# A decoder layer's expert gates: a table in HBM filled by indirect DMAs, in place of one-hot products

## The reference

```python
q = (xc @ wq).reshape(tc, H, 2, PEER_HALF)             # 8 heads, two halves of a key
s = einsum('thpd,hpnd->thpn', q, subkeys)               # 2 x 128 scores for a head and token
sv, si = top_k(s, K)                                    # 16 best of each half
cand = sv[:, :, 0, :, None] + sv[:, :, 1, None, :]      # 16 x 16 sums
cidx = si[:, :, 0, :, None] * NK + si[:, :, 1, None, :]
best, pos = top_k(cand, K)                              # 16 best pairs (i, j)
eidx = take_along_axis(cidx, pos, axis=-1)
gates = softmax(best)
act = gelu(einsum('td,thkd->thk', xc, u_tab[eidx]))
y = einsum('thk,thkd->td', gates * act, v_tab[eidx])
```

## Time and profile before

| | us |
|---|---|
| median of 3 runs | 1065.33 (1064.71 to 1065.81) |
| the profiled execution, its own time | 1063.1 |
| its span, first to last instruction | 1061.4 |
| PE busy | 1039.0 (98%) |
| DVE, ACT, POOL busy | 718.4, 520.2, 326.6 |
| HBM read, written | 202.15 MB, 2.10 MB |
| mean granted TensorE clock | 0.99 of full |

### The profile page before, as it was taken

The page is one execution under the profiler, slowest core; times in us unless marked ns, Lnnn a source line. Parts: engine busy times, 40 slices in busy tenths (PEclk is TensorE's granted clock), DMA queues, the critical chain, the costliest instruction groups (busy, mean ns, idle before and its releaser), DMA issues.

```text
span 1061.4 us, 18274 instructions
## 1 busy us (share of the span) xinstructions
PE 1039.0 (98%) x7154; PEld 963.8 (91%) x7154; DVE 718.4 (68%) x1601; ACT 520.2 (49%) x797; POOL 326.6 (31%) x161
## 2 busy tenths in 40 slices
PE   8999999889999999999999999999999999999996
PEld 8999889889999999999999999988888888888875
DVE  7778887964897069556666767765555756666556
ACT  5686657335444454544434343355544555455542
POOL 1000000001888788866666666600001000000002
PEclk9999999988999999999999999999999999999999
DMA  9878748544555555544444444456669567776651
GB/s 360 325 242 307 246 139 314 165 137 160 179 176 180 177 175 182 187 158 137 143 140 140 139 140 140 140 177 193 193 192 334 180 205 250 235 240 205 195 174 42
DMA packets 57413, 205.43 MB, mean 194 GB/s; under 512 B 6768, under 2 KB 8816, under 8 KB 56560
## 3 DMA queue, kind: packets, MB, share of 16 engines
q1 hardware_dynamic: 55616, 199.01, 57.0%
q0 software_dynamic: 1424, 5.24, 1.3%
q10 hardware_dynamic: 288, 0.01, 0.0%
HBM read 202.15 MB, written 2.10 MB: 192 GB/s over the span
## 4 chain that ended last, share of the span: by engine, by line
PE 91%; DVE 4%; ACT 1%; issue 1%; DMA 1%; SPq 0%; ACTq 0%; DVEq 0%
PE px L1079 33%; PE pw L786 16%; PE pw L787 16%; PE pw L788 15%; PE px L1051 5%; DMA ada<-in_ada 1%; DVE w_lo L1130 1%; PE px L1017 1%; PE px L786 1%; PE px L787 0%; PE px L788 0%; PE px L850 0%; ACT w_hi L487 0%; PE px L947 0%; PE pw L1099 0%
## 5 line engine op out<-in xcount | busy, mean ns | idle before, releaser
L487 ACT ACTIVATE w_hi<-raw 128x1024 fp32r<-128x1024 f32 x312 | 328.5, 1056 | 334.0 <-PE px L1079 168.8
L786 PE MATMUL pw<-a_hi,w_hi 128*128 128x256 f32 x1280 | 370.0, 289 | 2.1 <-DVE a_lo L1391 2.1
L787 PE MATMUL pw<-a_lo,w_hi 128*128 128x256 f32 x1280 | 362.6, 283 | 0.0
L788 PE MATMUL pw<-a_hi,w_lo 128*128 128x256 f32 x1280 | 362.5, 283 | 0.0
L420 POOL TENSOR_TENSOR w_lo<-raw,w_hi 128x1024 fp32r<-128x1024 f32 x128 | 307.5, 2403 | 142.2 <-ACT w_hi L487 140.9
L1130 DVE TENSOR_TENSOR w_lo<-raw,w_hi 128x1024 fp32r<-128x1024 f32 x184 | 224.5, 1229 | 156.0 <-ACT w_hi L487 155.3
L786 PEld LDWEIGHTS pw<-a_hi,w_hi 128*128 128x128 f32 x1280 | 245.8, 192 | 3.8 <-DVE a_lo L1391 2.5
L787 PEld LDWEIGHTS pw<-a_lo,w_hi 128*128 128x128 f32 x1280 | 246.1, 192 | 0.1
L788 PEld LDWEIGHTS pw<-a_hi,w_lo 128*128 128x128 f32 x1280 | 245.8, 192 | 0.0
L1079 PE MATMUL px<-w_hi,ws_hi 128*128 128x512 f32 x512 | 159.3, 390 | 0.9 <-DVE ws_lo L1543 0.9
L1079 PE MATMUL px<-w_lo,ws_hi 128*128 128x512 f32 x512 | 159.0, 389 | 0.0
(11 more groups left out here) (328 smaller groups left out, 1118.0 us busy)
## 6 DMA issues: line engine op xcount, KB each, us to landing
raw<-in_u SPq DMA_DIRECT2D x128, 512.0 KB, 3.7
raw<-in_v SPq DMA_DIRECT2D x128, 512.0 KB, 4.6
raw<-in_ws SPq DMA_DIRECT2D x56, 512.0 KB, 4.9
ada<-in_w_ada SPq DMA_DIRECT2D x32, 512.0 KB, 7.1
ada<-in_ada SPq DMA_DIRECT2D x6, 1024.0 KB, 11.1
raw<-in_w SPq DMA_DIRECT2D x7, 768.0 KB, 11.2
ada<-in_ada SPq DMA_DIRECT2D x4, 512.0 KB, 7.0
xT<-in_xT SPq DMA_DIRECT2D x8, 128.0 KB, 10.4
```

The costliest lines, as they stand in the source:

```text
L487: return nc.scalar.activation(out, in_, ACT.Copy, **kw)
L786: nc.tensor.matmul(out, lh, rh, start=start and x == 0, stop=False)
L787: nc.tensor.matmul(out, lh, rl, start=False, stop=False)
L788: last = nc.tensor.matmul(out, ll, rh, start=False, stop=stop and x == len(pairs) - 1)
```

## The change

The gates no longer pass through one-hot products. A table of 128 x 128 x 256 floats (16.8 MB) is kept in HBM, ordered j, i, token. POOL clears it in 32 DMAs of 512 KB from a zero tile of 256 floats a partition, each tied to a count of low parts made in the blocks. The place of a choice in the table is (j x 128 + i) x 256 + token; DVE works it out for each unit. The units go in another order (two heads of tile 0, then the same heads of tile 1), in groups of four, each with its exp. When the gates of a group are ready, POOL issues 64 indirect DMAs, one for each unit and each of the 16 choices: each adds 128 floats (one for a token) to their 128 places in the table, and a unit waits until the additions of the unit before of the same tile have landed. SP waits for all additions before it loads the first row of the table and the first piece of V; then each row of V brings a table row of 128 KB (128 runs of 1 KB) with it, in a ring of four. DVE multiplies it into the row of W (`gate_w`) ahead of the split.

POOL keeps the low parts of U's pieces 0 to 15. DVE makes those of 16 to 127; its unit is cut into six steps, and one low part goes ahead of each. ACT only runs gelus in U, with four exps, after groups 6, 20, 32 and 44. PE's one-hots and transposes are gone.

```diff
-GA_U = 31
-OH = T // 4
-SCORES_AFTER = (4, 8, 11, 15)
-ENDS_AFTER = (18, GA_U - 2)
+UNITS = TT * PH
+SCORES_AFTER = (7, 12, 17, 22)
+POOL_PIECES = 16
+PER_UNIT = 6
+EXP_AFTER = (6, 20, 32, 44)
+ZERO = 256
+ZERO_DMAS = 32
...
 
+            def load_gates(r):
+
+                if r >= RING:
+                    sp.wait_ge(w_gated, r - RING + 1)
+                sp.dma_start(g_row[:, r % RING], gates_d[r * P * T:(r + 1) * P * T].rearrange("(i t) o -> i (t o)", i=P)) \
+                    .then_inc(g_landed[r % RING], 16)
+
             for m in range(UP, VP + NK):
+                if m == VP:
+                    for t in range(TT):
+                        sp.wait_ge(scattered[t], 16 * PH * TOPK)
+                    for r in range(RING):
+                        load_gates(r)
                 load_piece(m)
                 r = m - VP
+                if r >= RING:
...
 
+            table = gates_d.rearrange("(n i f) o -> n i (f o)", i=P, n=ZERO_DMAS)
+
+            def clear(first, last):
+
+                for n in range(first, last):
+                    pool.wait_ge(lo_ready, 4 + 46 * n // ZERO_DMAS)
+                    pool.dma_start(table[n].rearrange("i (a f) -> i a f", f=ZERO),
+                                   zero[:, :].unsqueeze(1).broadcast_to([P, NK * T // ZERO // ZERO_DMAS, ZERO])) \
+                        .then_inc(zero_landed, 16)
+
+            pool.wait_ge(zero_ready, 1)
+            clear(0, 9)
             pool.wait_ge(aT_copied, TT)
             nc.gpsimd.affine_select(out=aT[:, :, :, :].rearrange("p a h t -> p (a h) t"),
                                     in_=aT[:, :, :, :].rearrange("p a h t -> p (a h) t"),
                                     compare_op=ALU.is_ge, fill=0.0, base=0,
                                     pattern=[[0, TT * HG], [1, P]], channel_multiplier=-1).then_inc(aT_ready, 1)
+            clear(9, 25)
 
             pool.wait_ge(mod2_done, 1)
             pool.wait_ge(gt1_done, 1)
             nc.gpsimd.memset(keys[:, :, :], 0.0).then_inc(keys_cleared, 1)
+            clear(25, 28)
 
             for t in range(TT):
                 pool.wait_ge(xn_ready[t], 2)
             pool.dma_start(x1_d.rearrange("(a p) n -> p a n", p=P), x1[:, :, :]).then_inc(x1_spilled, 16)
+            clear(28, ZERO_DMAS)
 
             pool.wait_ge(lo_ready, UP)
-            for m in range(UP, VP):
+            for m in range(UP, UP + POOL_PIECES):
                 split_lo(m)
 
+            pool.wait_ge(zero_landed, 16 * ZERO_DMAS)
+            for c in range(PH // 2):
+                pool.wait_ge(gate_ready, c + 1)
+                for h in range(2):
+                    for t in range(TT):
+                        if 2 * c + h:
+                            pool.wait_ge(scattered[t], 16 * TOPK * (2 * c + h))
+                        i = 4 * c + 2 * t + h
+                        for k in range(TOPK):
+                            nc.gpsimd.indirect_dma_start(gates_d, bass.IndirectOffsetOnAxis(ap=place[:, i, k:k + 1], axis=0),
+                                                         gate[:, i, k:k + 1], None, compute_op=ALU.add) \
+                                .then_inc(scattered[t], 16)
 
             pool.wait_ge(piece_used, VP + E_ROWS)
             pool.wait_ge(x1_spilled, 16)
...
 
 
-            for g in range(GA_U):
+            def split_w(v):
+
+                act.wait_ge(w_gated, v + 1)
+                if v >= RING:
+                    act.wait_ge(piece_used, VP + v - RING + 1)
+                copy(ws_hi[:, v % RING], W[:, v]).then_inc(wsplit_hi, 1)
+
+            for g in range(NG):
                 if g == 8:
                     act.wait_ge(x1_spilled, 16)
+                if g == NG - 1:
+                    for r in range(RING):
+                        split_w(r)
                 split_hi(UP + 2 * g + 4)
                 act.wait_ge(piece_used, UP + 2 * g + 2)
                 nc.scalar.activation(W[:, 2 * g:2 * g + 2], pw[g % 2][:, :].rearrange("p (j t) -> p j t", j=2), ACT.Gelu) \
                     .then_inc(u_out, 1)
                 split_hi(UP + 2 * g + 5)
-                for t in range(TT):
-                    if g == ENDS_AFTER[t] - 1:
-                        q = slice(t * PH, (t + 1) * PH)
-                        act.wait_ge(best_ready, t + 1)
+                for c in range(PH // 2):
+                    if g == EXP_AFTER[c]:
+                        q = slice(4 * c, 4 * c + 4)
+                        act.wait_ge(best_ready, c + 1)
                         nc.scalar.activation(gate[:, q], gate[:, q], ACT.Exp).then_inc(gate_exp, 1)
-                    if g == ENDS_AFTER[t]:
-                        act.wait_ge(idxT_done, t + 1)
...
@@ -1007,14 +1027,15 @@
                 after(b)
 
 
-            def scores(t, c):
-
-                if t == 0:
+            def scores(n):
+
+                c, t = divmod(n, TT)
+                if n < 4:
                     pe.wait_ge(act_took, evac_count(WQ + c))
                 else:
-                    pe.wait_ge(score_used, 2 * c + 2)
+                    pe.wait_ge(score_used, 2 * (n - 4) + 2)
                 for h in range(2):
-                    last = nc.tensor.matmul(px[c][:, h * T:(h + 1) * T], qpT[:, 2 * c + h, t * P:(t + 1) * P],
+                    last = nc.tensor.matmul(px[n % 4][:, h * T:(h + 1) * T], qpT[:, 2 * c + h, t * P:(t + 1) * P],
                                             keys[:, 2 * c + h], start=True, stop=True)
                 last.then_inc(score_done, 1)
 
...
-                    elif g - 2 < GA_U:
+                    else:
                         pe.wait_ge(u_out, g - 1)
-                    else:
-                        pe.wait_ge(u_gated, g - 1 - GA_U)
                 columns_piece(m, pw[g % 2][:, e * T:(e + 1) * T])
 
...
-            def one_hots(n):
-
-                pe.wait_ge(oh_ready, n + 1)
-                if n >= 4:
-                    pe.wait_ge(g_lower_taken, n - 3)
-                    pe.wait_ge(g_upper_taken, n - 3)
-                for y in range(4):
-                    last = nc.tensor.matmul(px[n % 4][:, y * P:(y + 1) * P], oh_i[n % 2][:, y], oh_j[n % 2][:, y],
-                                            start=True, stop=True)
-                last.then_inc(oh_used, 1)
...
-                scores(0, c)
-            for g in range(GA_U):
+            for n in range(4):
+                scores(n)
+            for g in range(NG):
                 for e in range(2):
                     u_piece(g, e)
                 if g in SCORES_AFTER:
-                    scores(1, SCORES_AFTER.index(g))
-                if g in ENDS_AFTER:
-                    transposed(ENDS_AFTER.index(g))
-            for g in range(GA_U, NG):
-                for e in range(2):
-                    u_piece(g, e)
-                    n = 2 * (g - GA_U) + e
-                    if n < OH:
-                        one_hots(n)
+                    scores(4 + SCORES_AFTER.index(g))
 
             def v_part(v, t, halves=(0, 1)):
 
...
+            def gates(c):
+
+                q = slice(4 * c, 4 * c + 4)
+                need(at["last"])
+                v.tensor_tensor(gate[:, q], best[:, q], best[:, q, 0:1].broadcast_to([P, 4, TOPK]), ALU.subtract) \
                     .then_inc(best_ready, 1)
+                for t in range(TT):
+                    ins = v.tensor_scalar(place_f[:, 2 * t:2 * t + 2], ij[:, 0, 4 * c + 2 * t:4 * c + 2 * t + 2], float(T),
+                                          token[:, t:t + 1], ALU.mult, ALU.add)
+                need(go(ins))
+                v.scalar_tensor_tensor(place[:, q], ij[:, 1, q], float(P * T), place_f[:, :, :], ALU.mult, ALU.add)
+
+            def normal(c):
+
+                q = slice(4 * c, 4 * c + 4)
+                dve.wait_ge(gate_exp, c + 1)
+                need(go(v.tensor_reduce(gsum[:, q], gate[:, q], AX, ALU.add)))
+                need(go(v.reciprocal(ginv[:, q], gsum[:, q])))
+                v.tensor_tensor(gate[:, q], gate[:, q], ginv[:, q].unsqueeze(2).broadcast_to([P, 4, TOPK]),
                                 ALU.mult).then_inc(gate_ready, 1)
 
+            dve.wait_ge(zero_landed, 16 * ZERO_DMAS)
+            for i in range(4):
+                for step in steps:
+                    step(i)
+            gates(0)
+            upper_half(4)
+            lower_half(4)
+            normal(0)
+            dve.wait_ge(lo_ready, UP + POOL_PIECES)
+            m = UP + POOL_PIECES
+            for i in range(4, UNITS):
+                for n, step in enumerate(steps):
+                    split_lo(m)
+                    m += 1
+                    if i > 4 or n > 1:
+                        step(i)
+                    if i > 4 and i % 4 == 0 and n == 4:
+                        normal(i // 4 - 1)
+                if i % 4 == 3:
+                    gates(i // 4)
+            while m < VP:
+                split_lo(m)
+                m += 1
+                if m == UP + POOL_PIECES + PER_UNIT * (UNITS - 4) + 5:
```

(64 more changed lines are left out.)

157 lines of the change are left out of this document (34 added, 123 removed).

## The result

The changed kernel takes **1206.37 us** (median of 4 runs, 1201.99 to 1208.31), against 1065.05 for the kernel before (4 runs, 1064.71 to 1065.81): a ratio of 1.132, 95% interval 1.1289 to 1.1352. The forecast of 1014 (1004 to 1024) was wrong, and so was its sign. It is rival 2, further out than I had priced it. The profiled execution took 1206.38 with a span of 1204.6.

A forecast was written before the change was run, and what follows sets the result against it. PE was taken as the bound, busy 98% of the span with 91% of the chain. 1063.1 - 57.4 (one-hots, transposes) + 3 (clears) + 3 (V) = 1011.7; the runs' median lies 2.2 higher: forecast 1014, range 1004 to 1024.

The forecast's parts named there:

- rival 2: SP's wait before V: scatter late, p over 1.43, V starting at 314.6 + 256 p + 12.5; 1108 to 1152; chance 0.28.
- The chain of work: In U, one-hots add plainly to PE's path; removing them and the transposes saves 57.4 us, and DVE's low parts fit.
- p: Time per indirect DMA that POOL issues for the scatter, 256 in all: taken as 1.0 us.
- My upper bound: Upper p for POOL's indirect DMAs: 0.88 for a plain DMA plus 0.89 of blocking by DVE, 1.77 us.
- The threshold: Before V: last issue over by 629.9, 12.5 us ahead of V's first matmul, allowing p up to 1.21 us.
- The clears: In the blocks before U, 32 DMAs of 512 KB clearing the table: cost taken as 3 us, between 0 and 11.
- V: In V, DVE's gate products and the table rows: cost taken as 3 us, between 0 and 15.
- The rule on the shared port: DVE and GpSimd share an SBUF port pair by exclusive lock, so each indirect DMA could wait out a low part.
- Rival 1: Before V: scatter late but still faster, p between 1.21 and 1.43; 1031 at p 1.3; chance 0.16.
- Rival 3: DVE in U or table rows in V set the cadence: 11 and 29 us, together 1024 to 1051; chance 0.07.
- Rival 4: On PE: the change brings nothing, its time being filled otherwise; within 0.2%, chance 0.03.

The follow-up runs named there:

- kernel 1: The changed kernel with every second of the 16 choices left out, so 128 indirect DMAs in place of 256: 1010.47 us.
- the second table: kernel 1 with a second table of the same size added, cleared beside the first and read by nobody: 1028.84 us.
- experiment 6: The changed kernel with VectorE's low parts for U's pieces 16 to 127 cut to 64 of 1024 columns: 1177.76 us.

## Why the prediction was wrong, point by point

**The chain of work was right.** One-hots were an addition to PE's stream: U fell from 429.2 to 372.0 us, against 429.2 less the forecast 57.4 = 371.8. PE waits for no low part in U, so VectorE carries 112 of them beside top-k, as worked out.

**The step that failed is p**, the price of an indirect DMA, taken as 1.0 and bounded at 1.77, with 1.21 as the most that the forecast could bear. It measured 1.965, and V's first matmul came at 835.25 instead of near 645. In parts, from the experiments: 0.97 for the DMA with 128 places and a plain write; 0.59 for the addition; 0.30 between two DMAs; and 0.10 for VectorE's low parts beside it (1.965 - 1.86). The plain DMAs of the earlier trace rows were the wrong neighbours in three ways. They gave 0.88, near the 0.97, but by size, and size is not what is paid. The addition was mentioned and not priced by itself. And the gap of 0.30 appears in no row of a lone DMA, so a string of them was priced without it. My upper bound put the blocking of the earlier trace rows on every DMA, which turned out nine times too much, and still fell short, since it had neither the addition nor the gap.

**The threshold was right.** The prediction asked for the last issue over by 629.9, thus started by some 628; the runs put the knee at a last start of 626.5 to 628. The 12.5 us from there to V's first matmul measured 13.0. With the measured price, rival 2's own formula gives V's start as 314.6 + 256 x 1.965 + 12.5 = 830.1, against 835.25 on the chip; 5 of that 5.15 are the first gates, ready at 319.7 in this execution, and 315.1 in kernel 1. The time by it would be 1063.1 + (830.1 - 699.8) + 6 + 2.2 = 1201.6, against 1206.37. So the rival was right in place and mechanism, and its formula gives the size once p is known; but it had a chance of 0.28, and its highest p of 1.77 gives only 1152.

The first 4 us, by which the first score is late (271.0 against 266.7), fit TensorE's clock. Between 10 and 20 us the granted clock was 0.57 here and 0.83 in the kernel before, with the same work (here, then before):

```profile
10.00:20.00 10.00, 7.73 (x39) 0.57 1.01 416
```

```profile
10.00:20.00 10.00, 7.55 (x50) 0.83 1.02 417
```

The kernel with ten choices had 0.58 there and kernel 1 had 0.83, with the same code up to that point, so it goes by the execution and not by the change. By 213 us that is 2.8 us (213.34 against 210.59 for the same matmuls, of L992 here and of L972 before). The other 1.6 arise between 210 and 250 us, where the clock was low again (0.51 from 240 to 250, where before had 0.73).

**The clears**, taken as 3 (0 to 11), cost nothing that shows (266.5 against 266.7). The count of idle DMA time was too strict, as if no ring of pieces absorbed anything, but it had the two places where the second table breaks through.

**V**, taken as 3 (0 to 15), cost 1.2 in kernel 1. In the changed kernel V's matmuls span 1193.1 - 835.2 = 357.9, 5.8 over before's 352.1. Two waits of PE are 2.5 of it. One, of 0.73 us at 955.83, ends a wait for a table row issued at 941.59, just behind the loads of the end's constants, as the prediction had feared. The other, of 1.72 at 985.04, stands behind late rows and 4.7 us of VectorE's arithmetic for the end. (The 0.86 still missing to 191.8 - 188.5 = 3.3 is the wait at V's last row, which the kernel before has too.) Another 2.7 fit the clock: after the hole the first matmuls of V run at the lower level:

```profile
835.25 1.19 PE L1069 MATMUL px<-w_hi,ws_hi 128*128 128x512 f32 x2 [188.54 <-DVE ws_lo L1552]
```

The granted clock was 0.51 over the hole, the 1.2 GHz level, and from this pair to the next it is 0.99 us (836.24), where two matmuls of V come to 0.45 in the earlier trace rows (2 x 307.39 / 1356). The first seven pairs take 5.89 us (to 841.14) instead of 7 x 0.453 = 3.17. What is left, 0.6, stays open.

**The rule on the shared port** (the Trainium skill, SBUF — State Buffer, "Who interferes with whom") was quoted as pointing to the upper p. The trace agrees in kind: experiment 6 shows VectorE's two-input operation lengthening GpSimd's DMAs. In size this does not carry the case: it is 24 us of the 246 by which 255 x 1.965 exceeds 255 x 1.0. And the other side of a lock, low parts held up by the DMAs, does not show: the longest low part takes 1227 ns.

**Rivals 1, 3 and 4** did not come about. Rival 1 needed p under 1.43, and even a plain write's was 1.46 on average ((687.0 - 315.3) / 255). Rival 3 needed VectorE or the table rows as a cadence; VectorE's low parts stayed at 1223 ns on average, and V without table rows is 1.1 us shorter. Rival 4 needed the removed one-hots to bring nothing; U is 57.2 us shorter.

## What to carry to other kernels

A DMA that an engine issues has a price in that engine's time, and for indirect ones it goes by their number: halving the elements of each took 7.5% off (1.72 against 1.86), halving their number left the price of each as it was (median 1557 ns). Before work is moved to such a queue, multiply the number of DMAs by a price measured back to back, the gap included, and hold it against the latest start that the waiting stage allows. Where the price has no row and the verdict turns on it, a lone plain DMA is no bound from above; and where the new path has room for only a part of the work, split the work between the new path and the old one. Since the price goes by the DMA, the obvious next thing is fewer DMAs with more places in each, several choices of a token in one; no run here tried it.

## What was not expected of the hardware

- Back to back in the hole, an indirect DMA issued by GpSimd takes 1.86 us with an addition of 128 four-byte places, 1.72 with 64; as a plain write 1.27 and 1.19. 0.30 of each is a gap before it in which the trace shows no wait.
- The hold-up goes one way here. GpSimd's indirect DMAs are stretched by VectorE's low parts from 1.56 up to 2.60 us, while these low parts stay at 1206 to 1227 ns throughout:

```profile
L1118 DVE TENSOR_TENSOR w_lo<-raw,w_hi x296: 1206/1225/1227, 54.9 to 1183.1; 128x1024 fp32r<-128x1024 f32 x148
```

  In the earlier trace rows it was the other way round: the select stretched the low part to 2112.
- The blocks hide 16.8 MB of writes for nothing and pay 18.4 us for the next 16.8. A DMA share of 0.97 from 60 to 100 us (kernel 1) and of 1.00 (the plain write, first score at 266.6) was still free, and 1.02 (two tables) was not.
